# Three token parts that each run norm, retention and projection on their own, with expert lookups hosted there

## The reference

```python
z = rms_norm(x, g_mix)
rq, rk, rv, aq, ak, av, ga, gb = jnp.split(z @ w_in, IN_SPLITS, axis=-1)
# retention: 4 heads, chunks of 128 tokens, a state of 128 x 256 per head carried from chunk to chunk
r_out, r_state = ret_fn(rotate(rq), rotate(rk), rv, log_decay)
# differential attention: 4 heads, causal over all earlier tokens
a_out = att_fn(partial_rotary(aq), partial_rotary(ak), av, lam)
m = sigmoid(ga) * (rms_norm(r_out) @ w_br_ret) + sigmoid(gb) * (norm(a_out) @ w_br_att)
h = x + m @ w_out
z2 = rms_norm(h, g_ffn)
# PEER: per token and each of 8 heads the best 16 of 128 x 128 = 16384 experts
ids, gate = top16_of_product_keys(z2 @ w_query, sub_keys)
f = sum_k gelu(z2 . expert_u[ids_k]) * gate_k * expert_v[ids_k]
y = rms_norm(h + f, g_final)
```

## Time and profile before

| | us |
|---|---|
| median of 3 runs | 4081.39 (4072.09 to 4085.74) |
| profiled execution, device time | 4082.75 |
| its span in the profile | 4081.0 |

### The profile page before, as it was taken

The page is one execution under the profiler, slowest core; times in us unless marked ns, Lnnn a source line. Parts: engine busy times, 40 slices in busy tenths (PEclk is TensorE's granted clock), DMA queues, the critical chain, the costliest instruction groups (busy, mean ns, idle before and its releaser), DMA issues. The chain is left out here.

```text
span 4081.0 us, 33096 instructions
## 1 busy us (share of the span) xinstructions
PE 3178.8 (78%) x10192; PEld 1855.6 (45%) x10192; DVE 2614.9 (64%) x5466; ACT 731.2 (18%) x1774; POOL 1243.7 (30%) x1030
## 2 busy tenths in 40 slices
PE   6997988767775856447867354899999999999994
PEld 3553436453442524113524254455555555555552
DVE  2221112088773888644846997678887888778876
ACT  1110011015221134011221054111111111111111
POOL 0000000033342322322422375334444444444442
PEclk9998998885797956669978677899999999999997
DMA  4002103327896234977963069999999999999996
GB/s 137 6 16 88 48 17 116 139 60 279 323 377 247 63 114 178 344 277 265 401 242 108 1 205 282 363 408 392 415 410 408 407 415 410 410 406 405 406 401 250
DMA packets 316820, 1044.53 MB, mean 256 GB/s; under 512 B 125523, under 2 KB 158435, under 8 KB 229603
## 3 DMA queue, kind: packets, MB, share of 16 engines
q0 software_dynamic: 95728, 687.91, 42.1%
q1 hardware_dynamic: 215522, 346.08, 23.9%
q10 hardware_dynamic: 5392, 8.42, 0.6%
HBM read 988.04 MB, written 54.29 MB: 255 GB/s over the span
## 5 line engine op out<-in xcount | busy, mean ns | idle before, releaser
L199 POOL DMA_INDIRECT lk_rows<-in_expert_uv,lk_ids x640 | 964.7, 1507 | 1590.6 <-DVE lk_sums L240 1492.2
L209 DVE SCALAR_TENSOR_TENSOR lk_rows<-lk_rows,lk_z_rows 128x1024 f32<-128x1024 f32 x648 | 784.9, 1228 | 252.8 <-DMA lk_rows<-in_expert_uv,lk_ids 237.4
L240 DVE SCALAR_TENSOR_TENSOR lk_sums<-lk_rows,lk_weights,lk_sums 128x1024 f32<-128x1024 f32 x647 | 829.8, 1283 | 37.9 <-DVE lk_sums L240 0.9
L2013 PE MATMUL ps<-zT_C,ex_u 128*128 128x384 f32 x2048 | 692.6, 500 | 88.4 <-DVE ex_a L2052 50.3
L2026 PE MATMUL ps<-ex_a,ex_v 128*128 128x384 f32 x2048 | 687.2, 496 | 60.2 <-DVE accT L2061 47.6
L2013 PEld LDWEIGHTS ps<-zT_C,ex_u 128*128 128x128 f32 x2048 | 400.1, 196 | 375.6 <-issue 79.0
L2026 PEld LDWEIGHTS ps<-ex_a,ex_v 128*128 128x128 f32 x2048 | 394.8, 194 | 347.5 <-DVE accT L2061 60.6
L217 ACT ACTIVATE lk_weights<-lk_weights 128x2 f32<-128x2 f32 x324 | 66.1, 204 | 1690.9 <-DVE lk_rows L209 1690.7
L1606 POOL MEMSET rtA_scores<- 128x128 f32 x2 | 0.4, 206 | 746.6 <-POOLq L86 746.6
L2061 DVE TENSOR_TENSOR accT<-accT,ps 128x384 f32<-128x384 f32 x248 | 126.4, 547 | 77.6 <-PE ps L2026 77.6
L1919 PE MATMUL ps<-ga_onehot_i,ga_onehot_j 128*128 128x128 f32 x768 | 105.1, 301 | 73.6 <-issue 63.2
(11 more groups left out here) (483 smaller groups left out, 3885.7 us busy)
## 6 DMA issues: line engine op xcount, KB each, us to landing
ex_u<-in_expert_uT SPq DMA_DIRECT2D x128, 512.0 KB, 14.8
ex_v<-in_expert_v SPq DMA_DIRECT2D x128, 512.0 KB, 12.1
gate_scratch<-ga_stage SPq DMA_DIRECT2D x6, 4096.0 KB, 29.5
ex_gates<-gate_scratch SPq DMA_DIRECT2D x128, 192.0 KB, 8.4
mgA_w<-in_w_merge SPq DMA_DIRECT2D x8, 1792.0 KB, 7.2
mgB_w<-in_w_merge SPq DMA_DIRECT2D x8, 1792.0 KB, 9.0
mgC_w<-in_w_merge SPq DMA_DIRECT2D x8, 1792.0 KB, 12.2
lk_rows<-in_expert_uv,lk_ids POOLq DMA_INDIRECT x640, 11.1
```

Source lines behind the costliest of these rows:

```text
L199: pool.indirect_dma_start(out=self.slot[:, s, :], out_offset=None, in_=self.a["expert_uv"], in_offset=bass.IndirectOffsetOnAxis(ap=index, ...
L209: self.nc.vector.scalar_tensor_tensor(out=u, in0=u, scalar=1.0, in1=self.z[:, t % 2, :], op0=ALU.mult, op1=ALU.mult, accum_out=self.w[:, t ...
L240: self.nc.vector.scalar_tensor_tensor(out=total, in0=v, scalar=w, in1=total, op0=ALU.mult, op1=ALU.add).then_inc(self.added, 1)
L2013: last = nc.tensor.matmul(ps[:, n % HB, 0:DENSE], U[:, n % UB, k, :], zD[:, k, :], start=(k == 0), stop=(k == KD - 1))
```

## The change

Norm, retention and attention projection now run once per part, so that each part goes through all its stages before the next one starts. `Part` gets stage numbers for `norm`, `ret` and `proj` and its own `KT` and `VA`. The retention state is one buffer kept from A to C. The weights `w_ret` and `w_att` are loaded in each part. Keys of earlier tiles go through a scratch in HBM (`kT_dram`) and values come back from the output `o_v_p`. The transfers of `zT` and `rT` of B and C through HBM are gone. In the norm stage the load of the first two weight blocks is issued after the second tile, the others after the last. The new stages of B and C host lookups: one batch per tile in norm, three per chunk in retention, three per tile (`HOSTED`) in projection.

```diff
@@ build @@
+        state = mem.place("ret_state", [P, RH, RDV], A.ret, C.ret)
...
+        for p in parts:
+            p.r = mem.place(f"rT_{p.name}", [P, KD, p.width], p.ret, p.merge)
+            p.KT = mem.place(f"KT_{p.name}", [P, AH, p.end * P], p.proj, p.att)
+            p.VA = mem.place(f"VA_{p.name}", [P, p.end, AH * ADV], p.proj, p.att)
...
         for p in parts:
             lookup = look if p is not A else None
-            attention_phase(nc, a, ps, ident, mem, p, late.get(p), KT, VA, lam, lookup)
+            with Scope(nc) as ret:
+                w_ret = mem.place(f"w_ret_{p.name}", [P, KD, WR], p.norm, p.ret)
...
+                norm_phase(nc, a, ps, ident, mem, p, lam, w_ret, w_ret_in, lookup)
+                retention_phase(nc, a, ps, ident, mem, p, state, rows_s, w_ret, w_ret_in, lookup)
+            attention_projection(nc, a, ps, ident, mem, p, kT_dram, rows_s, lookup)
+            attention_phase(nc, a, ps, ident, mem, p, lam, lookup)
@@ norm_phase: scalar, vector @@
                 nc.scalar.activation(junk[0:rows, :], x[0:rows, u, :], ACT.Square,
                                      accum_out=st[0:rows, u, 0:1]).then_inc(squared[u], 1)
+                if look and i:
+                    look.on_act(act)
                 act.wait_ge(mean[u], ONE + it + 1)
...
                     gain[:, :].unsqueeze(2).to_broadcast([P, KD, rows]), ALU.mult).then_inc(kept[u], 1)
+                if look:
+                    look.on_dve(dve)
@@ retention_phase: tensor @@
-            for t in range(NT - 1):
+            for t in range(M - 1):
                 chunk(t, lambda banks: project(t + 1, banks))
                 project(t + 1, range(2, PROJ))
                 turn_out(t)
-            chunk(NT - 1)
-            project(NT, range(PROJ), NS)
-            turn_out(NT - 1)
+            chunk(M - 1)
+            if HAS_ROWS:
+                project(M, range(PROJ), NS)
+            turn_out(M - 1)
@@ attention_projection: sync, vector @@
+            if T0:
+                sp.dma_start(KT[:, :, 0:LO], kT_dram[:, :, 0:LO]).then_inc(earlier, 16)
+                sp.dma_start(VA[:, 0:T0, :], a["o_v_p"][0:LO, :].rearrange("(t p) n -> p t n", p=P)).then_inc(earlier, 16)
...
+            else:
+                sp.wait_ge(kept, ONE + M)
+                sp.dma_start(kT_dram[:, :, LO:HI], KT[:, :, LO:HI]).then_inc(kept_back, 16)
+                sp.wait_ge(kept_back, ONE + 16)
...
-                nc.vector.tensor_copy(KT[:, :, t * P:(t + 1) * P],
+                nc.vector.tensor_copy(half.columns(KT[:, :, LO:HI], T0 + t),
                                       ps[:, 7, :].rearrange("p (h l) -> p h l", h=AH)).then_inc(kept, 1)
+                if look:
+                    look.on_dve(dve, HOSTED)
```

More of the change, by code:

```diff
@@ L124, in __init__ @@
         self.name, self.tiles = "ABC"[index], tiles
-        self.att, self.sample, self.merge, self.res, self.route = range(3 + 5 * index, 8 + 5 * index)
+        (self.norm, self.ret, self.proj, self.att, self.sample, self.merge, self.res,
+         self.route) = range(8 * index, 8 * index + 8)
         self.lo, self.width = tiles[0][1], sum(r for _, _, r in tiles)
@@ L130, in __init__ @@
         self.whole = [x for x in tiles if x[2] == P]
[L131 removed]
+        self.t0, self.end = tiles[0][0], tiles[0][0] + len(self.whole)
+        self.z = self.q = self.r = self.a = self.m = self.KT = self.VA = None
     def columns(self, buf, t, rows=P):
@@ L293, in build @@
         look_scope.start()
[L295 to L299, removed]
-        for p in reversed(parts):
-            p.q = mem.place(f"qT_{p.name}", [P, AH, P * len(p.whole)], PROJ, p.att)
+        kT_dram = dram("key_scratch", [P, AH, SEQ])
@@ L354, in norm_phase @@
             "columns_kept"))
+        tiles = [(i, i % 2, i // 2, *half.tiles[i]) for i in range(len(half.tiles))]
         block = ctx.block()
@@ L359, in _, with weights @@
         def _(sp):
-            for t, lo, rows in TILES:
-                u, it = t % 2, t // 2
+            def weights(b):
+                cols = slice(b * BANK, (b + 1) * BANK)
+                sp.dma_start(w_ret[:, :, cols], a["w_ret"][:, :, cols]).then_inc(w_ret_in[b], 16)
+            for i, u, it, t, lo, rows in tiles:
                 if it:
@@ L716, in _ @@
+            if T0:
+                sp.wait_ge(earlier, ONE + 32)
+            sp.wait_ge(k_stored, ONE + 16 * len(half.tiles))
+            sp.wait_ge(v_stored, ONE + 16 * len(half.tiles))
+        @block.gpsimd
+        def _(pool):
+            if look:
+                look.on_pool(pool, HOSTED * M)
         @block.tensor
@@ L742, in _ @@
             turn(0)
-            for t in range(2, NT):
+            for t in range(2, M):
                 project(t)
                 turn(t - 1)
-            project(NT, NS)
-            turn(NT - 1)
+            if HAS_ROWS:
+                project(M, NS)
+            turn(M - 1)
         @block.vector
@@ L766, in _ @@
             dve.wait_ge(s_tab, ONE + 32)
-            for t in range(NT):
+            for t in range(M):
                 u = t % 2
```

252 lines of the change are left out of this document (133 added, 119 removed).

## The result

| | median, us (lowest to highest) | ratio to before, 95% interval |
|---|---|---|
| before, beside the changed kernel | 4077.09 (4072.09 to 4085.74) | |
| changed | 4192.48 (4186.56 to 4196.36) | 1.0279 (1.0255 to 1.0304) |

A forecast was written before the change was run, and what follows sets the result against it. The long expert stage was taken as bound by transfers, early stages by TensorE and start-up. Three passes +101, hosting +106 and expert stage gain -120 give +87 us on 4082.75: 4170 us, range 4105 to 4255.

The forecast's parts named there:

- What bounds the kernel: Expert stage bound by transfers, DMA at 0.99 and 400 GB/s; with fewer picks TensorE is next.
- The gain: Expert stage shortens by 120 us, between 90 and 139, as 43 batches of picks leave it.
- The 15 us added for stalls: Expert stage: allowance for remaining stalls at a DMA load of 0.91, within the predicted 1356 us.
- The side calculation by the 358 GB/s: Expert stage: at that HBM rate 502 MB take some 1400 us and the gain is 80 us; chance 0.02.
- Three passes without picks: Entering norm, retention and projection three times costs +29, +36 and +46 us, about 10 back: +101 us.
- The cost of hosting: 43 batches hosted in norm, retention and projection of B and C cost 106 us, likely 60 to 160.
- Norm of B and C at 45 to 52 us each: Sign to look for: length of each norm stage of parts B and C with hosted picks.
- The bare bursts of projection: Projection of B: second burst delays the third turn some 18 us, third lies bare; 32 us with late weights.
- Table switches: ScalarE switches activation tables twice a tile, 1.28 us each, mostly covered; a drain would add 36 us.
- Faster: Picks vanish in VectorE's idle time, hosting under about 20 us with the usual gain; 4045 us, chance 0.08.
- Starved picks: Hosted batches take 7.2 us each as weights share the engines, perhaps a lower clock; 4269 us, chance 0.10.
- The expert stage hardly gains: VectorE's order, not rows, keeps TensorE waiting there; gain only 70 us, total 4220 us, chance 0.10.

The follow-up runs named there:

- experiment 1: Changed kernel with its three passes but no picks in norm, retention and projection; 4171.89 us, ratio 1.0230.
- experiment 6: Changed kernel with no picks in norm and only the covered bursts in projection, 27 batches moved; 4086.38 us, ratio 1.0012.
- experiment 7: Changed kernel, 27 batches in covered places, weights after rows, last four gathers left to the next hosting stage except in gates; 4082.41 us, ratio 1.0000.
- Experiment 2: Changed kernel with all four retention weight blocks issued after the last rows of x in norm; 4175.94 us, ratio 1.0239.
- experiment 3: Changed kernel with the last four gathers of each hosting stage left to the next one that hosts; 4189.25 us, ratio 1.0273.
- experiment 9: Kernel before with the last four gathers held back only in the residual stages of B and C; 4065.67 us, ratio 0.9972.
- experiment 4: Kernel before with the last four gathers of each hosting stage left to the next one that hosts; 4092.50 us, ratio 1.0034.

## Why the prediction was right, and where its sum was off

**Direction and time.** 4170 us were forecast, 4192.48 measured, inside the range. The three terms were +101 + 106 - 120 = +87; the spans give +100 + 142 - 138 = +104. The middle term lacked two waits, some 54 us, and was too large by some 18 us in what it did price (below). With the two waits and its own prices the forecast would have been 4224 us, still in the range; that 4170 lies only 22 us off is in part luck.

**What bounds the kernel.** Right. The expert stage was bound by transfers, and with 86 picks fewer TensorE is next (the earlier trace rows against the groups after).

**The gain.** Forecast 120, within 90 and 139; measured 137 to the last matmul (1480.4 to 1343.0), 138 to the end. Of the 137 only 127 go with the 43 batches: experiment 1 has 1469.8 us with none moved, and the other 10.6 us are spread between runs or come from the structure. The 15 us added for stalls were too much. At 0.93 of DMA the stage lies 22 us over TensorE's 1321. The side calculation by the 358 GB/s of the Trainium skill (DMA: Bandwidth & Descriptors, section Where 436 GB/s comes from) fell: experiment 1 moved 403 GB/s through the whole expert stage.

**Three passes without picks.** Forecast +101, measured +98.4 at the start of attention C (in experiment 1). From TensorE's start of one stage to that of the next the parts hold too: retention +48.7, where the forecast, with the two further weight loads (8.4 us each) counted there, has +53; projection +26.8 for +29; norm, with what comes back in attention, +22.9 for +19. In norm B some 4 us of it are the third tile's wait behind the weights, which the forecast didn't have (22.6 us in experiment 6, 18.5 in experiment 7 with the rows first). A chunk of retention stayed at 35.3 us (600.56 to 635.85 in B). This is the term of which one could be surest, since every piece of it stood in a row of before, and it is the one that alone undoes most of the gain.

**The cost of hosting.** This is the term that was mis-sized: 142 for 106, still inside its 60 to 160. Over half of the difference is norm of B, 40.8 for 21. Of the signs that the forecast named, "Norm of B and C at 45 to 52 us each" missed: from the stage's first issue to retention they take 71.7 and 57.5 us. The forecast took "rows land about 14 us after their issue" for the picks and added 9 us for the weights beside them. This is the first missing term: it looked at how long the picks' transfers take and not at what they and the order of SyncE's issues do to the third tile's rows, which stand behind two weight blocks. Experiment 2 took 16.5 us out by changing that order alone. The rest is spread over the other stages (+5 retention B, +4 projection B, +6.5 norm C, -2 and +1.5 in C).

The second missing term is the wait for gathers still in flight at a stage's end. From the last work of TensorE, VectorE or ScalarE to the next stage's first issue, changed kernel against experiment 1:

| | changed | without picks | difference |
|---|---|---|---|
| norm B | 13.20 | 4.05 | 9.15 |
| retention B | 13.13 | 4.43 | 8.70 |
| projection B | 12.86 | 7.07 | 5.79 |
| norm C | 15.06 | 4.34 | 10.72 |
| retention C | 4.45 | 5.12 | -0.67 |
| projection C | 12.65 | 6.02 | 6.63 |

That is 40 us of the 142. With the third tile's rows in norm B (24.27 us for 10.01, 14 us more) the two waits make some 54 us, so what the forecast did price came to some 88 us, where it has 106. It was thus too high on the batches themselves and had nothing for these waits, and the two errors partly cancelled.

The wait at the boundary was visible in before: the earlier trace rows gives 32.80 us before the output product with picks against 14.43 without, and it was read there as competition for the engines. The traces of before say otherwise. Of the 18.4 us, 8.8 are hosted work of VectorE after the last matmul of merge B (10.6 us for 1.8 in A), 10.2 are the boundary (last work to the first issue of `w_out` 13.4 us for 3.1), and the weights themselves came in 8.8 us for 9.5. The last work of merge B and the first issue behind it, in the kernel before:

```profile
1213.63 0.56 DVE L1380 TENSOR_TENSOR mT_B<-mgB_products 128x384 f32<-128x384 f32 x1
...
1227.55 1.26 SPq L1307 DMA_DIRECT2D w_outB<-in_w_out  x2
```

Since experiment 3 shortened the stages of norm, retention and projection of B by 14.0, 1.3 and 8.7 us and lengthened norm and retention of C by 11.9 and 8.4, how much of the 40 us can be saved stays open; most of it wasn't saved there.

**The bare bursts of projection.** Right in mechanism and size: "some 18 us" before the last turn in B. TensorE in B's projection:

```profile
782.64 1.04 PE L777 MATMUL ps<-ident,apB_qk 128*128 128x128 f32 x8
801.04 1.97 PE L777 MATMUL ps<-ident,apB_qk 128*128 128x128 f32 x8 [17.36 <-DVE apB_qk L807]
832.97 1.65 PE L903 MATMUL ps<-KT_B,qT_B 64*128 64x384 f32 x4 [29.96 <-PEq L85]
```

The 29.96 us behind it are the third burst (15.8 us on VectorE, 804.25 to 820.06) and the end of the stage.

**Table switches.** Right: a load of 1.28 us and the root at once behind it, on ScalarE in norm B. No drain shows, so the 36 us worked out beside the Trainium skill's page on ScalarE: Activation LUTs, section What ACT_TABLE_LOAD costs, did not come.

```profile
504.40 1.28 ACT L385 ACT_TABLE_LOAD   x1
505.69 0.20 ACT L385 ACTIVATE mixB_st<-mixB_st 128x1 f32<-128x1 f32 x1
```

**The rivals.** *Faster* needed hosting of all 43 batches under 20 us, and it cost 142; with only covered places (32 us for 27 batches) this structure reaches the time of before. *Starved picks* did not come as a rate: retention ran at a clock of 0.87 and 0.92 with chunks of 35.3 us; waits for transfers occurred at single points, above all the rows in norm B. *The expert stage hardly gains* fell.

## What to carry to other kernels

Moving work out of a transfer-bound stage pays only until the next engine binds it: here 5.6 us a batch for the first 18, 0.5 for the last 16. Compute that number first and then fill only places where another engine has work of its own in the same moment; idle engine time in a chain (norm) or at a stage's end is not cover. And splitting a stage costs its start and end once more for every pass, a price that can be read off the profile before and set against the gain.

Where stages are separated by barriers, stop prefetching for the next one early enough that nothing is in flight at the barrier, but only if the stage that will fetch it instead doesn't begin on loads of its own. Here that was worth 12 us of 4078 where it paid (experiment 9), and it cost 15 us where it was done everywhere (experiment 4).

## What the runs showed of the hardware

The end of a stage followed the landing of gathers already issued, though no instruction of the stage used their rows: 13.2 us from the last work with them, 4.1 without, at the end of norm B. It is the landing that it followed: the next stage's first issue came 4.6 us after the last landing in the changed kernel and in experiment 2 at the end of norm B (11.1 and 13.8 us after the issue's end), and 4.4 us after it in both at the end of norm C (13.0 and 13.8). What in the stage's end waits for it, these runs don't show.

A short load behind large ones on SyncE was late: 0.5 MB landed 37 us after its issue began, behind 4.2 MB of weights and beside seven gathers, and the issue itself held SyncE for 18.93 us. Without the gathers (experiment 1) it landed after 13.7 us, and the issue took 2.72. TensorE's granted clock stood at 0.50, its lower level of 1.2 GHz, through both norms, where it has 2 us of transposes a tile, and at 1.00 through the expert stage, where TensorE was idle for 15 of 1343.5 us, for 0.96 before, where it was idle for 111 of 1480.0.
